# Hybrid attention and expert block on one core: where the attention bias table is skewed, and which engine masks it

## What is computed

```python
s_win = einsum('bhqd,bhqkd->bhqk', q, k_window) * scale + rel_bias[:, dr, dc]   # dr, dc: row and column offset of key and query
s_ctx = einsum('bhqd,bhkd->bhqk', q, k_ctx) * scale
p = softmax(concatenate([s_win, s_ctx]))
```

## Time and profile before

| | before |
|---|---|
| median of 3 runs | 1540.67 us |
| lowest, highest run | 1536.49, 1540.75 us |
| span of the profiled execution, first to last instruction | 1534.0 us |
| its mean granted TensorE clock | 0.966 |
| busy: TensorE, VectorE, ScalarE, GpSimd | 1411.7 (92%), 906.6 (59%), 685.4 (45%), 247.3 us (16%) |
| DMA traffic | 348.00 MB, 227 GB/s on average |

### The profile page before, as it was taken

How to read it: one execution, slowest core, us unless ns; L and a number is a source line. 1 busy time by engine, 2 the same in 40 slices (tenths; PEclk the granted TensorE clock), 3 DMA queues, 4 the chain that set the end, 5 groups by cost and what they waited for, 6 DMA issues and landing times.

```text
span 1534.0 us, 17969 instructions
## 1 busy us (share of the span) xinstructions
PE 1411.7 (92%) x7076; PEld 977.7 (64%) x7076; DVE 906.6 (59%) x1200; ACT 685.4 (45%) x961; POOL 247.3 (16%) x211
## 2 busy tenths in 40 slices
PE   4999999998999976999999889989978997999997
PEld 1786567645888854777777568876837994343333
DVE  2567983855744446988888634976487763112112
ACT  2654452346233345777777446443336552101002
POOL 0006970600000001112110030084140000000000
PEclk9899999999999987999999959999989998999999
DMA  9611006793131535999999882111743755999990
GB/s 356 237 55 55 23 33 163 249 389 132 55 110 56 219 135 187 378 400 397 395 393 404 326 299 100 40 59 54 217 159 148 298 215 205 422 423 410 425 416 34
DMA packets 96461, 348.00 MB, mean 227 GB/s; under 512 B 21744, under 2 KB 22896, under 8 KB 84080
## 3 DMA queue, kind: packets, MB, share of 16 engines
q1 hardware_dynamic: 92704, 333.76, 57.2%
q0 software_dynamic: 2976, 10.49, 2.1%
q10 hardware_dynamic: 688, 2.49, 0.4%
HBM read 337.29 MB, written 9.44 MB: 226 GB/s over the span
## 4 chain that ended last, share of the span: by engine, by line
PE 51%; DVE 4%; ACT 2%; issue 2%; DMA 1%; POOL 1%; DVEq 0%; POOLq 0%
PE bank L1383 7%; PE bank L1405 4%; PE bank L1118 4%; PE bank L1115 4%; PE bank L1124 4%; PE bank L803 2%; PE bank L1144 2%; PE bank L1154 2%; PE bank L705 2%; PE bank L1149 2%; PE bank L1416 2%; PE bank L1362 1%; PE bank L761 1%; PE bank L941 1%; PE bank L943 1%
## 5 line engine op out<-in xcount | busy, mean ns | idle before, releaser
L2920 DVE TENSOR_TENSOR slab_lo<-slab,high 128x4096 fp32r<-128x4096 f32 x48 | 210.8, 4418 | 4.9 <-ACT high L2057 4.9
L2057 ACT ACTIVATE high<-slab 128x4096 fp32r<-128x4096 f32 x48 | 174.1, 3631 | 21.3 <-PE bank L1124 19.4
L2343 POOL DMA_INDIRECT feed_rows<-token_table,slot_token x16 | 44.9, 2805 | 475.2 <-DVE slot_token L2861 285.3
L1383 PE MATMUL bank<-narrow_slab,picked 128*64 128x512 f32 x256 | 112.5, 592 | 0.2 <-ACT picked L2223 0.2
L1384 PE MATMUL bank<-narrow_slab,picked 128*64 128x512 f32 x256 | 112.5, 592 | 0.0
L803 PE MATMUL bank<-hT,ring 128*128 128x512 f32 (+1 forms) x256 | 104.0, 545 | 0.0
L2212 ACT ACTIVATE gated<-bank 64x512 f32<-64x512 f32 x16 | 9.4, 589 | 166.6 <-PE bank L1384 166.6
L1383 PEld LDWEIGHTS bank<-narrow_slab,picked 128*64 128x64 f32 x256 | 35.0, 137 | 67.4 <-issue 66.9
L3085 DVE TENSOR_TENSOR hidden<-bank,gated 64x512 f32<-64x512 f32 x16 | 17.0, 1064 | 94.0 <-ACT gated L2212 94.0
L2300 POOL TENSOR_TENSOR pair<-pf 128x512 f32<-128x512 f32 (+1 forms) x32 | 34.4, 1076 | 223.3 <-DVE pb L2545 216.5
L1405 PE MATMUL bank<-narrow_slab,hiddenT 128*64 128x512 f32 x256 | 58.5, 597 | 11.2 <-issue 11.2
(11 more groups left out here) (413 smaller groups left out, 3208.3 us busy)
## 6 DMA issues: line engine op xcount, KB each, us to landing
ring<-in_w_ada SPq DMA_DIRECT2D x24, 2048.0 KB, 13.5
ring<-in_w_in SPq DMA_DIRECT2D x24, 2048.0 KB, 10.3
slab<-in_w_gate SPq DMA_DIRECT2D x16, 2048.0 KB, 14.2
slab<-in_w_up SPq DMA_DIRECT2D x16, 2048.0 KB, 14.6
slab<-in_w_down SPq DMA_DIRECT2D x16, 2048.0 KB, 14.9
narrow_slab<-in_w_gate SPq DMA_DIRECT2D x16, 2048.0 KB, 14.4
narrow_slab<-in_w_up SPq DMA_DIRECT2D x16, 2048.0 KB, 12.0
narrow_slab<-in_w_down SPq DMA_DIRECT2D x16, 2048.0 KB, 10.0
```

Source lines behind the costliest of these rows:

```text
L1383: T.matmul(bank[0][0:64, :], x, gate[:, k, :], start=(k == 0), stop=(k == KT - 1))
L2057: S.activation(half_of(e, kind)[:], w[:], ACT.Copy)\
L2343: G.indirect_dma_start(feed_rows[e % 2][0:DEALT, :], None, token_table, bass.IndirectOffsetOnAxis(ap=slot_token[0:DEALT, e:e + 1], axis=0))\
L2920: V.tensor_tensor(low[:], w[:], half_of(e, kind)[:].bitcast(f32), ALU.subtract)\
```

## The change

The skew is done from DRAM to DRAM: a DRAM table `skew_table` of 2 MB a layer is filled by 64 transfers (both layers) with the same reads as before, issued by SP at the start, ahead of its wait for the slot of `("in", 0, 0)`. At the old place each layer has one transfer of 2 MB from that table to `bias_skew`, in which each partition reads 16 KB in a row. GpSimd's 16 instructions a layer are gone; VectorE does the same 16 (`window_bias(h)`, two for each head, the second after a wait for the first), behind `row_low(2, 5)` (heads 0 and 1), `row_low(2, 6)` (heads 2 and 3) and `row_low(2, 7)` (heads 4 to 7).

```diff
@@ SP @@
                     if loads[n] == ada_loads[(6, 22)[l]]:
 
                         sp.wait_ge(*is_ready(("o", l, HG_HEADS - 1)))
-                        for r in range(4):
+                        sp.wait_ge(sem["skew_stored"], 16 * 4 * NA_HEADS * DEPTH)
+                        sp.dma_start(bias_skew[:].rearrange("p h q c -> p (h q c)"), skew_table[l]).then_inc(sem["bias_loaded"], 16)
+                    if loads[n] == ("in", 0, 0):
+                        for layer, r, h in itertools.product(range(DEPTH), range(4), range(NA_HEADS)):
                             src = A["rel_bias_reversed"]
-                            for h in range(NA_HEADS):
-                                skew = bass.AP(src.tensor, ((l * NA_HEADS + h) * 15 + 7 - r) * 31 + 15 + 1 - GRID_W,
-                                               [[1, GRID_W], [31, 4], [1, GRID_W]])
-                                sp.dma_start(bias_skew[64 * (r % 2):64 * (r % 2) + 64, h, r // 2, :]
-                                             .rearrange("p (a c) -> p a c", a=4), skew).then_inc(sem["bias_loaded"], 16)
+                            skew = bass.AP(src.tensor, ((layer * NA_HEADS + h) * 15 + 7 - r) * 31 + 15 + 1 - GRID_W,
+                                           [[1, GRID_W], [31, 4], [1, GRID_W]])
+                            at = (h * 2 + r // 2) * 4 * GRID_W
+                            sp.dma_start(skew_table[layer, 64 * (r % 2):64 * (r % 2) + 64, at:at + 4 * GRID_W]
+                                         .rearrange("p (a c) -> p a c", a=4), skew).then_inc(sem["skew_stored"], 16)
@@ GpSimd @@
-                pool.wait_ge(sem["const_loaded"], 16)
-                pool.wait_ge(sem["bias_loaded"], 16 * 32 * (l + 1))
-                for h in range(NA_HEADS):
-                    b = bias[:, h].rearrange("p q (r c) -> p (q r) c", c=GRID_W)
-                    x = bias_skew[:, h].rearrange("p q (r c) -> p (q r) c", c=GRID_W)
-                    back = bass.AP(x.tensor, x.offset + GRID_W - 1, [x.ap[0], [GRID_W, 8], [-1, GRID_W]])
-                    wide = [P, 8, GRID_W]
-                    G.tensor_tensor(b, back, wmul.unsqueeze(1).to_broadcast(wide), ALU.mult).then_inc(sem["pool_chain"], 1)
-                    pool.wait_ge(sem["pool_chain"], 8 * l + h + 1)
-                    G.tensor_tensor(b, b, wneg.unsqueeze(1).to_broadcast(wide), ALU.add).then_inc(sem["bias_ready"], 1)
@@ VectorE @@
-                for s, ks in ((2, range(4)), (7, range(3)), (2, range(4, KT))):
-                    for k in ks:
-                        row_low(s, k)
+                def window_bias(h):
+                    if h == 0:
+                        dve.wait_ge(sem["bias_loaded"], 16 * (l + 1))
+                    b = bias[:, h].rearrange("p q (r c) -> p (q r) c", c=GRID_W)
+                    x = bias_skew[:, h].rearrange("p q (r c) -> p (q r) c", c=GRID_W)
+                    back = bass.AP(x.tensor, x.offset + GRID_W - 1, [x.ap[0], [GRID_W, 8], [-1, GRID_W]])
+                    wide = [P, 8, GRID_W]
+                    link(V.tensor_tensor(b, back, wmul.unsqueeze(1).to_broadcast(wide), ALU.mult))
+                    V.tensor_tensor(b, b, wneg.unsqueeze(1).to_broadcast(wide), ALU.add).then_inc(sem["bias_ready"], 1)
+
+                for k in range(4):
+                    row_low(2, k)
+                for k in range(3):
+                    row_low(7, k)
+                for k in range(4, KT):
+                    row_low(2, k)
+                    for h in ((), (0, 1), (2, 3), (4, 5, 6, 7))[k - 4]:
+                        window_bias(h)
```

More of the change, by code:

```diff
@@ L22 @@
+import itertools
 import numpy as np
@@ L295, in build @@
     token_table = nc.dram_tensor("token_table", (TOK, D), f32, kind="Internal").ap()
+    skew_table = nc.dram_tensor("skew_table", (DEPTH, P, NA_HEADS * 8 * GRID_W), f32, kind="Internal").ap()
     expert_table = nc.dram_tensor("expert_table", (N_EXPERTS * DEALT, D), f32, kind="Internal").ap()
-    names = """const_loaded vec_loaded x_loaded tables_loaded bias_loaded out_stored psum_ready side_ready blanks_ready cond_ready
+    names = """const_loaded vec_loaded x_loaded tables_loaded skew_stored bias_loaded out_stored psum_ready side_ready blanks_ready cond_ready
         pick2_ready ada_row ada_mod
@@ L313, in build @@
         chunk_high chunk_low row_over way_high way_low tile_high tile_low head_high head_low
-        dve_chain pool_chain""".split()
+        dve_chain""".split()
     with ExitStack() as ctx:
```

## The result

| | before | changed |
|---|---|---|
| median (6 runs each) | 1539.91 us | 1530.81 us |
| lowest, highest | 1536.49, 1543.78 us | 1527.31, 1531.85 us |
| span of the profiled execution | 1534.0 us | 1526.6 us |
| mean granted TensorE clock | 0.966 | 0.968 |

The ratio is 0.9938, with a 95% interval of 0.992 to 0.9956. Forecast was 1529.8 us, in a range of 1524.0 to 1536.5. The profiled execution of the changed kernel took 1528.73 us for a span of 1526.6, so only 2.1 us lie around the instructions. The 6.7 us that the prediction put there were mostly the distance of the profiled execution from the median: its span of 1534.0 belongs near the lowest run.

The account below looks back on a forecast made before the run. TensorE, 92% busy, was taken as the bound, idling for late rope in layer 1. Terms 0 (start) + 0 (layer 0) + 10.9 (layer 1): 1540.67 - 10.9 = 1529.8 us, range 1524 to 1536.5.

Parts of the forecast that it names:

- What bounds: Layer 1, attention start: TensorE, 92% busy, idles 9.56 us for rope's last piece, then slow groups cost 2.7 us.
- Why rope was late: Layer 1: GpSimd's instructions running beside rope make VectorE's instructions with both inputs in SBUF take 2.5 times as long.
- The sum for layer 1: Rope at full speed lets TensorE's second modulation group start at 1124.3 instead of 1135.17: gain 10.9 us.
- remaining wait for `probs`: Layer 1, after the third scores: TensorE still waits 1.8 us for VectorE to finish the first pair's scaling.
- The masks on VectorE: Values stage, layer 1: 1.33 us a pair of instructions, table there at 1092.6, VectorE done at 1104.5, hidden in idle time.
- the cover is thin: Layer 1: a table 1 us later moves the attention's start by 0.4 us, each further one by 1 us.
- Layer 0 and the start: Layer 0's masks and the 64 transfers at the start are both hidden: 0 us each.
- the stated 86 to 99: Start, SP's list: the 64 transfers take 42.3 us to issue, ending at 86 or 99 depending on the counted start.
- From there on nothing differs but the shift: After layer 1's attention start, everything merely moves earlier, so the 10.9 us gain reaches the end.
- The time around the instructions: Whole kernel: 6.7 us lie between the span and the median, added to the forecast span of 1523.1.

Follow-up runs that it names:

- the two needless loads: The changed kernel plus 16 unused GpSimd instructions a layer: multiplications reading two SBUF inputs, 1539.83 us; or memsets that only write, 1527.1 us.
- masks_more: The changed kernel with the mask multiplication of heads 4 to 7 done three times on VectorE: 1532.02 us, ratio 0.9958 to the kernel before.
- add_only: The changed kernel without the 16 mask multiplications, so VectorE only adds wneg: 1528.2 us, ratio 0.994 to the kernel before.
- store_twice: The changed kernel with every skew transfer done twice, 128 at the start instead of 64: 1541.53 us, ratio 1.0016 to the kernel before.
- the second measurement: The changed kernel unchanged, measured again for five rounds: 1528.92 us, ratio 0.9929 to the kernel before.

## Why the prediction was right, and where it was not

- *What bounds*: right. The 9.56 us of idle and the slow groups behind it are gone, and the granted clock between 1116 and 1135 is 1.00.
- *Why rope was late*: right, and shown by the two needless loads: reads on GpSimd bring the stretching back, writes do not.
- *The sum for layer 1*: 10.9 us forecast for the second modulation group, 10.8 measured in the profile (11.5 if the 0.65 us by which the execution came later are taken off). The remaining wait for `probs` was 1.35 us where I had 1.8. That rope ended at 1116.96 where 1117.0 was forecast is partly luck: I had it begin at 1104.5, held up by the masks, but these were done at 1103.25, and it began at 1104.24, when ScalarE's high half was there, in an execution that came 0.65 us later to the stage.
- *The masks on VectorE*: 1.33 us a head forecast, 1.34 measured; the table was used from 1091.32 on where I had 1092.6, in an execution that came 0.65 us later, so it was 1.9 us quicker than forecast: the two `ada` blocks ahead landed by 12.9 us after their issue instead of 14.1, and from 1085 to 1088 the DMA moved 453 GB/s where I had reckoned with 386. That the cover is thin was right: 5.8 us more of masks made the kernel 3.8 us slower (`masks_more` against `add_only`).
- *Layer 0 and the start*: nothing forecast, nothing seen. The 64 transfers ended at 95.3, inside the stated 86 to 99. Writing 256-byte pieces to DRAM went at 98 GB/s with a DMA share of about 0.6 (`store_twice`, 60 to 140 us), as writing them to SBUF had the earlier trace rows. The Trainium skill ("DMA: Bandwidth & Descriptors", Specifications) has transfers under 512 bytes done as read-modify-write; no price of that for DRAM over SBUF shows in these runs. No run tried larger pieces.
- *"From there on nothing differs but the shift"*: this step failed in the profiles, where 3.1 us of 10.5 are lost again in the expert stage to half clock. The medians, 9.1 us and in the second measurement 9.5 apart, are 1.4 to 1.8 us short of the forecast 10.9, but the interval of the ratio (6.8 to 12.3 us) takes in 10.9, so they do not show a shortfall by themselves. What decides whether the short idle times of that stage lower the clock stays open: the same gaps did it in ten profiles and not in three. The size of the gain does not sort them, nor does one edit alone; that all ten have the early table, the masks on VectorE or both does, but no run was made to test it.
- *The time around the instructions*: I took 6.7 us from one profile against a median of three; it is 2.1. The error did not change the difference; the profiled execution of the kernel before lay near the lowest time.

No version clearly beats the changed one: `add_only` has the same ratio within the intervals. It is the safer kernel, with 6.5 us of idle time ahead of rope instead of 1.0.

## What to carry to other kernels

When an engine that "has nothing else to do" is late, compare the lengths of its own instructions over time before looking for more work to take away: a length that jumps by 2.5 times and back, in step with GpSimd, points to a contention and not to a load. Then ask where the offending work can lie so that it overlaps nothing; here an earlier table alone gave half the gain, a table and half the work on the same engine gave all of it, and moving the work without the table cost 15 us. In these profiles a part of a gain was lost again to the clock in a later stage whose instructions the change never touched; so measure the end, not the stage.

## What was new about the hardware

- VectorE with one input in PSUM is not stretched by GpSimd (0.41 us beside reads, 0.42 alone), with two in SBUF it is (0.42 to 1.40, 0.69 to 1.67), and 16 GpSimd memsets of 0.54 us each stretch nothing.
- One transfer of 2 MB from a DRAM table with 16 KB a partition landed 11.3 us after its issue, behind 4 MB; the 32 that gather it in 256-byte pieces took 21 to 23 us to issue alone. Issued one behind the other, 0.66 to 0.71 us each, such transfers went at 95 to 101 GB/s, to SBUF and to DRAM alike. That the issue is the limit is inferred from the DMA share of about 0.6, not tested.
